# Filler products of the ones matrix in four of TensorE's waits in the delta rule layer

## The chip, the core and the metric

The kernel runs on one NeuronCore of a Trainium2 chip. The metric is the device time of one execution in microseconds (us). PE is TensorE (matrix products), DVE is VectorE, ACT is ScalarE, POOL is GpSimd, SP is the engine that issues the transfers. PSUM has eight banks of 128 partitions x 512 f32 values; PE writes its results there and the other engines read them.

## The reference, cut to what matters

Batch 1, 512 tokens, model width 1024. Three blocks follow each other: a gated delta rule and retention block with an MLP behind it, an attention and pooling block, and a convolution block. The change lies in the first.

```python
n = _rms_norm(h, attn_norm_w)
proj = einsum('bsd,dc->bsc', n, w_in)
(gq, gk, gv, gg, ga, gb, rq, rk, rv, rg) = split(proj)
o_gdn = _gated_deltanet(gq, gk, gv, gg, ga, gb, ...)   # conv, silu, l2norm, then per chunk:
    # m     = strict_lower((k*beta) k^T * decay);  t_mat = (I + m)^-1
    # qk    = (q k^T) * decay
    # u     = t_mat vb - w state;  o = q_dec state + qk u
    # o     = rms(o) * norm_w * silu(gate)
o_ret = _retention(rq, rk, rv, rg)
h = h + concat([o_gdn, o_ret]) @ w_out
```

## The kernel before

Activations are kept by feature, 128 features on the partitions and 512 tokens in a row. A *unit* u is one output tile of 128 features (or, for units 12 to 15, of 128 tokens by 512 columns) of one of the weight matrices, all units of all layers in one numbered list. Units 0 to 31 (U1 to U2) are the projection w_in of the first block, units 32 to 39 (U2 to U3) its w_out. A unit has two halves of four contraction tiles k each. `three` makes an f32 product of a tile from three products of rounded parts (w_hi x_hi, w_hi x_lo, w_lo x_hi), so a unit is 24 products of 128x512, lines 1799, 1800 and 1801. Weights come by DMA into `raw`, ACT rounds them to `w_hi` (line 662) and POOL takes the rest as `w_lo` (line 536), in a ring that PE's finished halves (`half_done`) release.

Everything runs in an order written out by hand for each engine; engines wait for each other by semaphores. The main products go to PSUM banks 0 to 3 (unit u to bank u % 4) and PE waits for `bank_free` before it writes one again. Banks 4 to 7 are for the small products of the delta rule and of retention, which PE does between two units. What matters here:

- After unit 12 (`u == 12`, line 2101) PE waits for `sqk`, ACT's squares of q and k (line 770), and sums them over features with the matrix ONES into banks 4 to 7.
- After unit 15 and after unit 16 (line 2119) it forms k k^T and then k q^T, 16 products of 128x128 each. Ahead of the second it waits for `m_ready`, with which DVE signals that it has read the first out of banks 4 to 7 (line 1382).
- DVE multiplies the second result by the decay (line 1350, `qkt_ready`), and makes the start matrix t of the inversion (lines 1354 and 1355, `t2_ready`). After unit 17 PE waits for both and transposes t (line 2126). ACT copies it (line 804), and six `level` steps between units 18 to 23 build the inverse.
- The tiles of units 12 to 15 are read by DVE at line 1376, with four increments of `bank_free`, ahead of the matrix m.
- The first four units of w_out are interleaved by the rule for QUADS: first the first halves (k = 0 to 3, the retention features) of all four, then the second halves (k = 4 to 7, the delta rule's heads). After the first of the first halves PE sums the squares of the four delta rule heads into banks 4 to 7 (`deltanet_ssq`, line 1823). ACT makes 1/rms of each (lines 859 and 860, one increment of `rr_ready` for each head, after two of the retention part), DVE applies it and the gate (lines 1410, 1414), ACT rounds the operand (line 673, `op_hi`) and DVE takes the rest (line 1180, `op_lo`). The second half of unit 32 waits for `op_hi` and `op_lo` of each k.

The kernel already has, further on at line 2259, 22 products of ONES with itself into bank 6, ahead of the convolution layer.

Of the kernel before, what the change touches and what calls it, by code (L numbers as in the profile page):

```python
# [9 lines left out]
P = 128  # L10
# [4 lines left out]
H = 4  # L15
# [34 lines left out]
U1, U2, U3, U4, U5, U6, U7, U8 = 0, 32, 40, 84, 108, 126, 134, 158  # L50
# [73 lines left out]
def build(nc, a, const, out, x_t):  # L124
    ctx = ExitStack()
    with ctx:
        base = (nc.sbuf_base + 31) // 32 * 32

        def at(name, shape, dt, off):
            return nc.alloc_sbuf_tensor_at(name, shape, dt, offset=base + off)  # L130

        def sem(name):
            return ctx.enter_context(nc.semaphore(name))
# [9 lines left out]
        ONES = at("ones", [P, P], F32, G + 512)  # L143
# [114 lines left out]
        PS = ctx.enter_context(nc.psum_tensor("ps", [P, 8, S], F32))  # L258
# [12 lines left out]
        bank_free = sem("bank_free")  # L271
# [30 lines left out]
        rsq_ready, rssq_filled, rr_ready = sem("ret_sq"), sem("ret_ssq_filled"), sem("ret_rstd")  # L302
# [1486 lines left out]
        def _(pe):  # L1789
            mm, tr = nc.tensor.matmul, nc.tensor.transpose  # L1790
# [6 lines left out]
            def three(out, w_hi_, w_lo_, x_hi_, x_lo_, first, last):  # L1797

                mm(out, w_hi_, x_hi_, start=first, stop=False)  # L1799
                mm(out, w_hi_, x_lo_, start=False, stop=False)  # L1800
                return mm(out, w_lo_, x_hi_, start=False, stop=last)  # L1801

            def half_unit(n, out, X, k0, kn, first, last, fill=None, later=None):


                for s_ in (w_hi, w_lo):
                    pe.wait_ge(s_, n + 1 if later is None else later + (n + 1))
                for k in range(kn):
                    if fill is not None:
                        operand(8 * fill + k0 + k)  # L1810
                    ins = three(out, WH[:, n % 4, k, :], WL[:, n % 4, k, :],
                                X[:, k0 + k, 0, :], X[:, k0 + k, 1, :],
                                first and k == 0, last and k == kn - 1)
                ins.then_inc(half_done, 1)

            def deltanet_ssq():

                pe.wait_ge(tokk_ready, 4)
                pe.wait_ge(tokv_ready, 16)
                pe.wait_ge(o_ready, 4)  # L1820
                for h in range(H):
                    pe.wait_ge(rsq_ready, 1 + h + 1)
                    mm(PS[:, 4 + h, :], ONES[:, :], RR[:, h, :], start=True, stop=True).then_inc(rssq_filled, 1)

            def four_halves(m, X, fill, k0):

                for k in range(2):
                    operand(8 * fill + k0 + k)
                    for j in range(4):
                        if k == 0:  # L1830
                            if k0 == 0:
                                pe.wait_ge(bank_free, m + j - 3)
                            pe.wait_ge(w_hi, 2 * U7 + k0 + j + 1)
                            pe.wait_ge(w_lo, 2 * U7 + k0 + j + 1)
                        three(PS[:, (m + j) % 4, :], WH[:, j, k, :], WL[:, j, k, :],
                              X[:, k0 + k, 0, :], X[:, k0 + k, 1, :], k0 + k == 0, False)
                for j in range(4):
                    if k0 == 4 and j == 3:
                        pre1_stat()
                    for k in range(2, 4):  # L1840
                        if j == 0:
                            operand(8 * fill + k0 + k)
                        ins = three(PS[:, (m + j) % 4, :], WH[:, j, k, :], WL[:, j, k, :],
                                    X[:, k0 + k, 0, :], X[:, k0 + k, 1, :], False, k0 + k == KT - 1)
                    ins.then_inc(half_done, 1)

            def unit(u, m, X, fill=None, later=None, mlater=None, midway=None):
                for q in QUADS:
                    if 0 <= u - q < 4:
                        if u == U7:  # L1850
                            four_halves(m, X, fill, 0)
                            four_halves(m, X, fill, 4)
                        if q == U7:
                            return
                        if u == q:
                            for j in range(4):
                                if m >= 4:
                                    pe.wait_ge(bank_free, m + j - 3)
                                half_unit(2 * q + j, PS[:, (m + j) % 4, :], X, 0, 4, True, False,
                                          fill if j == 0 else None)  # L1860
                                if j == 0 and u == U2:
                                    deltanet_ssq()
                            if midway is not None:
                                stat(midway)
                        half_unit(2 * q + 4 + u - q, PS[:, m % 4, :], X, 4, 4, False, True,
                                  fill if u == q else None)
                        return
                if m >= 4:

                    pe.wait_ge(bank_free, m - 3 if mlater is None else mlater + (m - 3))  # L1870
                out = PS[:, m % 4, :]
                half_unit(2 * u, out, X, 0, 4, True, False, fill, later)
                half_unit(2 * u + 1, out, X, 4, 4, False, True, fill, later)

            def wide_half(n, X, fill=None, last_of=None):

                q0 = max(q for q in WIDE if q <= n // 2)
                k = n - 2 * q0
                m = q0 if q0 < U2 else M8 + q0 - U8
                for s_ in (w_hi, w_lo):  # L1880
                    pe.wait_ge(s_, n + 1)
                if fill is not None:
                    operand(8 * fill + k)
                w, wl = (r[:, n % 4, :, :].rearrange("p t c -> p (t c)") for r in (WH, WL))
                for b in range(NB):
                    if k == 0:
                        pe.wait_ge(bank_free, m + b - 3)
                    xh, xl = (X[:, k, q, b * P:(b + 1) * P] for q in range(2))
                    ins = three(PS[:, (m + b) % 4, :], xh, xl, w, wl, k == 0, k == KT - 1)
                    if k == KT - 1 and b < NB - 1 and last_of is not None:  # L1890
                        ins.then_inc(last_of, 1)
                ins.then_inc(half_done, 1)

            def stat(st):

                pe.wait_ge(acc_done, squares_before(st) + 8)
                mm(PS[:, 7, :], ONES[:, :], ACC[:, :], start=True, stop=True).then_inc(stat_filled, 1)
# [164 lines left out]
            def ret_ssq(r):  # L2062
# [4 lines left out]
                    ins = mm(PS[:, 4 + h, :], ONES[:, :], RR[:, 2 * r + h, :], start=True, stop=True)  # L2067
                ins.then_inc(rssq_filled, 1)

            for u in range(U1, U2):  # L2070
                if 12 <= u < 16:
                    wide_half(2 * u, XA)
                    wide_half(2 * u + 1, XA)
                else:
                    unit(u, u, XA, fill=0 if u == 0 else None, midway=0)
                if u == 3:
                    pe.wait_ge(ab_split, 2)
                    pe.wait_ge(rstd_ready, 1)
                    for k in range(KT):
                        ins = three(PS[0:8, 7, :], ABH[:, k, :], ABL[:, k, :], XA[:, k, 0, :], XA[:, k, 1, :],  # L2080
                                    k == 0, k == KT - 1)
                    ins.then_inc(ab_filled, 1)
# [83 lines left out]
            for k in range(KT):  # L2166
                unit(U2 + k, M2 + k, XA, fill=1 if k == 0 else None)

            unit(U3, M3, XB, fill=2)
            pe.wait_ge(rr_ready, 2 + H)  # L2170
            stat(1)
# [56 lines left out]
            for u in range(U5, U6):  # L2228
                n = u - U5
# [150 lines left out]
```

## Time and profile before

| | us |
|---|---|
| three timed runs | 1213.53, 1218.21, 1221.34 |
| their median | 1218.21 |
| the profiled execution | 1210.9 |
| its span on the core | 1208.8 |
| PE busy | 1153.3 |
| DVE busy | 737.4 |
| POOL busy | 527.3 |
| ACT busy | 463.8 |

All times in the rows are from the profiled execution, counted from the start of its span. A product's duration in a row (0.39 us for 128x512) overlaps with the next one's; what one costs is the distance between two starts. A product of f32 operands that aren't rounded shows as two records. An idle time in square brackets stands with the row that ends it. PEclk is the TensorE clock that was granted, as a share of 2.4 GHz: 1.00 is 2.4 GHz, 0.50 is 1.2 GHz. The mean over this execution is 0.991.

### The profile page before, as it was taken

How to read it: one execution, taken by the hardware profiler on the slowest of the kernel's cores; microseconds unless marked ns; L12 is line 12 of the kernel's file. 1: busy time of each engine (PE TensorE's matmuls, PEld its weight loads, DVE VectorE, ACT ScalarE, POOL GpSimd, SP SyncE). 2: the span in 40 equal slices, each digit the busy share in tenths (PEclk: the TensorE clock that was granted, in tenths of full speed). 3: DMA queues.
4: the chain of work that ended last, by engine and by line, in shares of the span. 5: the costliest groups of instructions: out<-in, count | busy, mean ns of one | idle time of the engine just before them, and what ended most of it. 6: DMA issues, size and time to landing. Idle time of an engine off the chain costs nothing.

```text
span 1208.8 us, 16113 instructions
## 1 busy us (share of the span) xinstructions
PE 1153.3 (95%) x5876; PEld 918.8 (76%) x5876; DVE 737.4 (61%) x948; ACT 463.8 (38%) x812; POOL 527.3 (44%) x376
## 2 busy tenths in 40 slices
PE   5999999999989999999999999999989989999996
PEld 4686778877868777777778888876667768888774
DVE  5796664442356788888883111625764578886963
ACT  4325411215465333232232333434354443343553
POOL 4456520212225455545555444532237367532533
PEclk9999999999999999999999999999999999999998
DMA  8774341205213233233232323422123242122221
GB/s 270 102 88 71 48 57 36 36 1 140 70 35 105 70 105 104 70 103 104 71 103 95 97 96 99 145 71 69 35 70 85 55 123 71 35 71 71 70 70 70
DMA packets 101630, 99.37 MB, mean 82 GB/s; under 512 B 4804, under 2 KB 96069, under 8 KB 101061
## 3 DMA queue, kind: packets, MB, share of 16 engines
q1 hardware_dynamic: 101572, 98.59, 30.4%
q8 instruction: 38, 0.62, 0.2%
q14 instruction: 20, 0.16, 0.0%
HBM read 94.38 MB, written 4.19 MB: 82 GB/s over the span
## 4 chain that ended last, share of the span: by engine, by line
PE 61%; issue 15%; DVE 10%; POOL 9%; ACT 3%; DMA 1%; DVEq 0%; POOLq 0%; SPq 0%; ACTq 0%
PE ps L1799 15%; PE ps L1800 15%; PE ps L1801 15%; POOL w_lo L536 8%; PE ps L2276 4%; PE ps L2006 2%; PE ps L1999 2%; PE ps L2214 1%; PE ps L1968 1%; PE ps L2224 1%; PE ps L1989 1%; DVE conv L1637 1%; DVE v L1233 1%; PE ps L2101 1%; PE ps L1963 1%
## 5 line engine op out<-in xcount | busy, mean ns | idle before, releaser
L536 POOL TENSOR_TENSOR w_lo<-raw,w_hi 128x512 fp32r<-128x512 f32 x332 | 470.0, 1428 | 638.7 <-ACT w_hi L662 638.4
L662 ACT ACTIVATE w_hi<-raw 128x512 fp32r<-128x512 f32 x332 | 197.4, 618 | 231.2 <-PE ps L1801 209.2
L1799 PE MATMUL ps<-x_a,w_hi 128*128 128x512 f32 x624 | 253.1, 406 | 14.5 <-POOL w_lo L536 5.5
L1800 PE MATMUL ps<-x_a,w_hi 128*128 128x512 f32 x624 | 244.8, 392 | 0.0
L1801 PE MATMUL ps<-x_a,w_lo 128*128 128x512 f32 x624 | 244.6, 392 | 0.0
L1799 PE MATMUL ps<-x_b,w_hi 128*128 128x512 f32 x416 | 165.4, 398 | 2.7 <-POOL w_lo L536 1.4
L1801 PE MATMUL ps<-x_b,w_lo 128*128 128x512 f32 x416 | 162.3, 390 | 0.0
L1800 PE MATMUL ps<-x_b,w_hi 128*128 128x512 f32 x416 | 162.0, 389 | 0.0
L1799 PEld LDWEIGHTS ps<-x_a,w_hi 128*128 128x128 f32 x624 | 118.1, 189 | 54.8 <-issue 24.3
L1801 PEld LDWEIGHTS ps<-x_a,w_lo 128*128 128x128 f32 x624 | 118.1, 189 | 25.4
L1800 PEld LDWEIGHTS ps<-x_a,w_hi 128*128 128x128 f32 x624 | 118.3, 190 | 25.0 <-issue 2.2
L1799 PEld LDWEIGHTS ps<-x_b,w_hi 128*128 128x128 f32 x416 | 78.0, 188 | 30.5 <-issue 13.4
L1801 PEld LDWEIGHTS ps<-x_b,w_lo 128*128 128x128 f32 x416 | 78.1, 188 | 16.8
L1800 PEld LDWEIGHTS ps<-x_b,w_hi 128*128 128x128 f32 x416 | 78.1, 188 | 15.5 <-issue 0.2
L1637 DVE TENSOR_TENSOR conv<-ps,conv 32x511 f32<-32x511 f32 (+2 forms) x96 | 65.5, 682 | 17.2 <-ACT conv L1055 14.3
L1450 DVE SCALAR_TENSOR_TENSOR conv_f<-pad_f,mlp_conv,conv_f 128x512 f32<-128x512 f32 x44 | 67.6, 1536 | 6.5 <-DVE conv_f L1449 1.7
L1799 PE MATMUL ps<-mlp_act,w_hi 128*128 128x512 f32 x176 | 68.6, 390 | 0.2 <-POOL w_lo L536 0.2
L1801 PE MATMUL ps<-mlp_act,w_lo 128*128 128x512 f32 x176 | 68.5, 389 | 0.0
L1800 PE MATMUL ps<-mlp_act,w_hi 128*128 128x512 f32 x176 | 68.5, 389 | 0.0
L1472 DVE TENSOR_TENSOR res<-ps,res 128x512 f32<-128x512 f32 x8 | 5.5, 685 | 82.2 <-PE ps L1801 82.2
L1452 DVE SCALAR_TENSOR_TENSOR conv_f<-pad_f,mlp_conv,conv_f 128x512 f32<-128x512 f32 x44 | 51.6, 1173 | 6.3
L900 ACT ACTIVATE mlp_act<-prod_f 128x512 f32 (+1 forms) x22 | 13.9, 632 | 95.2 <-DVE prod_f L1459 95.2
(346 smaller groups left out, 1652.4 us busy)
## 6 DMA issues: line engine op xcount, KB each, us to landing
raw<-in_w_up SPq DMA_DIRECT2D x44, 512.0 KB, 4.3
raw<-in_w_in SPq DMA_DIRECT2D x32, 512.0 KB, 8.0
raw<-in_c_w_in SPq DMA_DIRECT2D x24, 512.0 KB, 4.6
raw<-in_a_w_in SPq DMA_DIRECT2D x18, 512.0 KB, 4.4
raw<-in_w_down SPq DMA_DIRECT2D x16, 512.0 KB, 4.3
raw<-in_w_out SPq DMA_DIRECT2D x8, 512.0 KB, 4.4
raw<-in_c_w_out SPq DMA_DIRECT2D x8, 512.0 KB, 4.2
raw<-in_w_down SPq DMA_DIRECT2D x8, 384.0 KB, 3.4
```

The costliest lines, as they stand in the source:

```text
L536: nc.gpsimd.tensor_tensor(ring_half(WL, n), raw_half(n), f32(ring_half(WH, n)), SUB) \
L662: nc.scalar.activation(ring_half(WH, n), raw_half(n), ACT.Copy).then_inc(w_hi, 1)
L900: nc.scalar.activation(ACTS[:, bass.ds(n + (j - 2), 1), 0, :] .rearrange("p a s -> p (a s)"), PRODF[:, j - 2, :], ACT.Copy) \
L1450: step(v.scalar_tensor_tensor(out=d, in0=x[:, 2:2 + S], scalar=w[1], in1=d, op0=MUL, op1=ADD))
L1452: ins = v.scalar_tensor_tensor(out=d, in0=x[:, 1:1 + S], scalar=w[0], in1=d, op0=MUL, op1=ADD)
L1637: ins = v.tensor_tensor(y, PS[32 * q:32 * q + 32, 4 + r, 0:S - late_by], y, ADD)
L1799: mm(out, w_hi_, x_hi_, start=first, stop=False)
L1800: mm(out, w_hi_, x_lo_, start=False, stop=False)
L1801: return mm(out, w_lo_, x_hi_, start=False, stop=last)
L1999: ins = mm(PS[:, 4 + c, h * 64:(h + 1) * 64], M[:, a_, :], half(TT[:, a_, :], 1), start=True, stop=True)
L2006: ins = mm(PS[:, 4 + c, 256 + h * 64:256 + (h + 1) * 64], T[:, a_, :], half(XZ[:, c, h, :], 1), start=True, stop=True)
L2276: ins = mm(PS[:, 4 + r, :], w, g[p, k % 2, TAP_PHASES * j:TAP_PHASES * j + S], start=first, stop=last)
```

## The change

At four places PE gets products of ONES[128x128] with ONES[128x128] ahead of a wait that it had: nine after unit 12 into bank 4, nine after unit 16 into bank 1, eleven after unit 17 into bank 2, and nine into bank 7 between the first and the second halves of the first four units of w_out. No engine reads the results; the next product into the same bank overwrites them. The two in the banks of main products wait for `bank_free` first, as the next unit does, and the last waits for `rr_ready` to reach 2 + H = 6, since bank 7 holds the fourth head's sum until ACT has taken it.

```diff
--- before.py
+++ after.py
@@ -1860,6 +1860,10 @@
                                           fill if j == 0 else None)
                                 if j == 0 and u == U2:
                                     deltanet_ssq()
+                            if u == U2:
+                                pe.wait_ge(rr_ready, 2 + H)
+                                for _ in range(9):
+                                    mm(PS[:, 7, 0:P], ONES[:, :], ONES[:, :], start=True, stop=True)
                             if midway is not None:
                                 stat(midway)
                         half_unit(2 * q + 4 + u - q, PS[:, m % 4, :], X, 4, 4, False, True,
@@ -2067,12 +2071,21 @@
                     ins = mm(PS[:, 4 + h, :], ONES[:, :], RR[:, 2 * r + h, :], start=True, stop=True)
                 ins.then_inc(rssq_filled, 1)
 
+            def ones_products(n, bank):
+                for _ in range(n):
+                    mm(PS[:, bank, 0:P], ONES[:, :], ONES[:, :], start=True, stop=True)
+
             for u in range(U1, U2):
                 if 12 <= u < 16:
                     wide_half(2 * u, XA)
                     wide_half(2 * u + 1, XA)
                 else:
                     unit(u, u, XA, fill=0 if u == 0 else None, midway=0)
+                if u == 12:
+                    ones_products(9, 4)
+                if u == 16 or u == 17:
+                    pe.wait_ge(bank_free, u + 1 - 3)
+                    ones_products(9 if u == 16 else 11, (u + 1) % 4)
                 if u == 3:
                     pe.wait_ge(ab_split, 2)
                     pe.wait_ge(rstd_ready, 1)
```

Two of the places in PE's own order, since the diff doesn't show what stands around them. In a row: line, operation, what it writes and reads, columns, and in brackets the semaphores that it waits for. `ret_rstd` is the program's name of `rr_ready`. PE between the halves of w_out's first units, with the change:

```order
L1799 MATMUL ps<-x_a,w_hi 128x512
L1800 MATMUL ps<-x_a,w_hi 128x512
L1801 MATMUL ps<-x_a,w_lo 128x512
L1866 MATMUL ps<-ones 128x128 [waits ret_rstd]
L1866 MATMUL ps<-ones 128x128 x8
L1799 MATMUL ps<-x_a,w_hi 128x512 [waits op_hi,op_lo,w_lo_ready,w_hi_ready]
L1800 MATMUL ps<-x_a,w_hi 128x512
L1801 MATMUL ps<-x_a,w_lo 128x512
L1799 MATMUL ps<-x_a,w_hi 128x512 [waits op_lo,op_hi]
```

The second halves of the products, k = 4 and on, now stand behind the nine and behind their wait. PE at the end of unit 17, with the change:

```order
L1801 MATMUL ps<-x_a,w_lo 128x512
L2076 MATMUL ps<-ones 128x128 [waits bank_free]
L2076 MATMUL ps<-ones 128x128 x10
L2139 MATMUL ps<-ident,t 128x128 [waits t2_ready,qkt_ready]
L2139 MATMUL ps<-ident,t 128x128 x15
```

Here the eleven stand ahead of the transposes (line 2126 before, 2139 with the change) and of their wait; nothing else has another place.

## Rows read from the trace of the kernel before

**Rows 1.** The page, busy time of PE, share of the span, instructions.

```profile
PE 1153.3 (95%) x5876; PEld 918.8 (76%) x5876; DVE 737.4 (61%) x948; ACT 463.8 (38%) x812; POOL 527.3 (44%) x376
```

**Rows 2.** Stretches: busy time (x count) by engine, PEclk, DMA share, GB/s.

```profile
core 0: us, PE busy (x) PEld busy (x) DVE busy (x) ACT busy (x) POOL busy (x), PEclk, DMA share, GB/s
104.30:109.50 5.20, 3.15 (x9) 1.48 (x9) 0.72 (x5) 4.22 (x7) 0.00 (x0) 1.00 0.99 151
143.20:145.40 2.20, 0.00 (x0) 0.00 (x0) 2.20 (x2) 0.63 (x1) 2.20 (x3) 1.00 0.00 0
146.60:149.70 3.10, 3.10 (x16) 3.10 (x16) 0.00 (x0) 0.00 (x0) 1.27 (x2) 0.50 0.96 87
149.70:150.60 0.90, 0.90 (x9) 0.90 (x9) 0.00 (x0) 0.00 (x0) 0.00 (x0) 0.95 0.97 96
156.40:159.00 2.60, 0.00 (x0) 0.03 (x1) 2.60 (x2) 0.00 (x0) 0.31 (x1) 1.00 0.79 77
160.00:163.50 3.50, 3.50 (x14) 3.11 (x13) 3.35 (x7) 1.77 (x2) 0.00 (x0) 0.51 0.00 0
356.60:362.00 5.40, 3.26 (x15) 2.55 (x15) 3.35 (x5) 1.93 (x4) 1.42 (x2) 1.00 0.58 194
951.00:958.00 7.00, 6.35 (x50) 5.86 (x49) 5.04 (x6) 3.67 (x6) 2.30 (x2) 1.00 0.01 2
```

**Rows 3.** Timeline of PE at full clock: start us, us, engine, line, what.

```profile
134.00 3.73 PE L2119 MATMUL ps<-kq 128*128 128x128 f32 x32
137.49 0.48 PE L1799 MATMUL ps<-x_a,w_hi 128*128 128x512 f32 x1
...
174.93 0.48 PE L1799 MATMUL ps<-x_a,w_hi 128*128 128x512 f32 x1
...
176.40 0.40 PE L1799 MATMUL ps<-x_a,w_hi 128*128 128x512 f32 x1
...
180.51 1.91 PE L1989 MATMUL ps<-ident,tt 128*128 128x128 f32 x16
182.25 3.68 PE L1999 MATMUL ps<-tt,m 128*128 128x64 f32 x32
...
951.15 5.07 PE L2259 MATMUL ps<-ones 128*128 128x128 f32 x44
```

**Rows 4.** Timeline of PE, ahead of and behind the first three waits.

```profile
103.86 0.39 PE L1801 MATMUL ps<-w_hi,x_a 128*128 128x512 f32 x1
106.34 3.70 PE L2101 MATMUL ps<-sq,ones 128*128 128x512 f32 x8 [2.09 <-ACT sq L770]
...
142.80 0.39 PE L1801 MATMUL ps<-x_a,w_lo 128*128 128x512 f32 x1
145.45 5.47 PE L2119 MATMUL ps<-kq 128*128 128x128 f32 x32 [2.26 <-DVE m L1382]
150.67 0.47 PE L1799 MATMUL ps<-x_a,w_hi 128*128 128x512 f32 x1
...
155.99 0.39 PE L1801 MATMUL ps<-x_a,w_lo 128*128 128x512 f32 x1
159.01 2.68 PE L2126 MATMUL ps<-ident,t 128*128 128x128 f32 x16 [2.63 <-DVE t L1355]
161.34 0.77 PE L1799 MATMUL ps<-x_a,w_hi 128*128 128x512 f32 x1
...
163.78 0.39 PE L1799 MATMUL ps<-x_a,w_hi 128*128 128x512 f32 x1
```

**Rows 5.** Timeline of DVE, the reads of the banks of units 12 to 15.

```profile
135.33 2.72 DVE L1376 TENSOR_SCALAR ret_v<-ps,rstd_col 128x512 f32<-128x512 f32 x4
```

**Rows 6.** Timeline at the second halves of w_out: ACT, PE and DVE.

```profile
354.21 0.63 ACT L860 ACTIVATE rr<-rr 128x512 f32<-128x512 f32 x1
354.90 0.39 PE L1799 MATMUL ps<-x_a,w_hi 128*128 128x512 f32 x1
...
357.91 1.47 DVE L1180 SCALAR_TENSOR_TENSOR x_a<-kq,x_a 128x512 fp32r<-128x512 f32 x2
358.75 0.47 PE L1799 MATMUL ps<-x_a,w_hi 128*128 128x512 f32 x1 [2.14 <-ACT x_a L673]
```

## The prediction

> **What bounds the kernel now.** I read the page's busy times first, then TensorE's (PE's) waits, then the granted clock around the long waits, then the rows of PE, DVE and ACT at the four places that the change touches. PE is busy for 1153.3 of 1208.8 us [rows 1], so it sets the end, and every microsecond that it loses or wins in a row of its own goes through to the end unless a later wait absorbs it. The four places that the change touches are waits of it [rows 4, 6]: 2.09 us for ACT's squares of q and k (call it place A, unit 12), 2.26 us for DVE's matrix m (B, unit 16), 2.63 us for DVE's matrix t (C, unit 17), and 2.14 us for the x_a operand after the gated norm (D, first unit of the output projection). In each of them PE stands while another engine works through a chain. The change puts products inside the waits; it doesn't shorten what is waited for. So nothing can come from the 9.1 us of waiting itself.
>
> What can come is the clock. The stretches of [rows 2] show it: at A and D the granted clock stays at 1.00 (2.4 GHz) during and behind the wait. At B the wait of 2.2 us is followed by 3.1 us at 0.50 (1.2 GHz), at C the wait of 2.6 us by 3.5 us at 0.51. (At A and D the stretch of the row holds the wait and some 3 us behind it.) The fall comes about 1 us after PE has started again, so the whole of it is paid in PE's own rows.
>
> **The change, part by part.** It adds 38 products of 128x128 by 128x128 (9, 9, 11, 9) and three waits ahead of them, and removes nothing.
>
> *Price of one product.* The kernel already has 22 such products: 44 records (an f32 product takes two) in 5.07 us, all at clock 1.00 [rows 2, 3]. 5.07 / 44 = 0.115 us for a record, so nine products take 18 x 0.115 = 2.07 us and eleven 22 x 0.115 = 2.53 us.
>
> *Are they hidden?* A: PE's last product before the wait starts at 103.86 [rows 4] and products of this form start 0.23 us apart, so the nine run from 104.09 to 106.16; the wait ended at 106.34. Spare 0.18 us. B: last start 142.80, so 143.03 + 2.07 = 145.10 against 145.45, spare 0.35. C: last start 155.99, so 156.22 + 2.53 = 158.75 against 159.01, spare 0.26. All three cost nothing, because ACT's and DVE's work covers them; without that cover they would cost their 2.07 or 2.53 us.
>
> *The added waits.* B and C wait for bank_free at 14 and at 15. The increments 13 to 16 come from DVE's four rows at L1376, which start at 135.33 and take 2.72 us together [rows 5]: done at 138.05, 5 us before PE comes to B. Price nothing. D waits until rr_ready has reached 6, which is ACT's fourth exponential at L860, 354.21 + 0.63 = 354.84 [rows 6]. PE reaches that point at 354.90: the start of k = 4 of the second half, which needs only the first head's operand. So this wait costs 0 to 0.1 us. Behind it stand the nine products, to 357.0, and only then k = 4 and k = 5, which before ran in the same gap (six products: six starts 0.23 us apart, with up to 0.1 us more where k = 5 waits anew, 1.5 us). They end at 357.0 + 1.5 = 358.5. The next row, k = 6, waited until 358.75 for DVE's L1180 (start 357.91). Spare 0.2 us, cost nothing. No other engine's work hangs on k = 4 and k = 5 alone, since the half's end is signalled after k = 7.
>
> *What the clock gives back at B.* The 32 records of L2119 take from 145.45 to the next row's start at 150.67, 5.22 us; the same 32 at unit 15 take 134.00 to 137.49, 3.49 us, at full clock [rows 3, 4]. Saving 1.73 us. DVE's L1350 starts on the end of these, and L1354 and L1355, for which C waits, follow it without a gap; so C's wait ends 1.73 us earlier too and stays as long as it was. The saving goes through.
>
> *What it gives back at C.* The 16 transposes of L2126 take 2.33 us to the next row's start, the 16 of L1989 at full clock 1.74: 0.59 us. The six products behind them take 161.34 to 163.78, 2.44 us, and six at full clock 174.93 to 176.40, 1.47 us: 0.97 us [rows 3, 4]. Saving 1.56 us. Behind it PE runs without a gap to the levels, whose DVE work is started by PE's own rows; short waits on DVE there move with PE. The weights' splits are released by PE's finished halves and move as well.
>
> *Do these products hold the clock?* Through the 22 of them, from 951 us on, and 2 us behind, the clock stayed at 1.00 [rows 2, 3]. At B it even rose again, to 0.95 as a mean from 149.7 us on, while PE ran only L2119, 128x128 f32 records of the same shape. I take it that they do. That they only help in part is bounded by nothing regained (0) and all (3.29).
>
> The Trainium skill (TensorE: Matmul & The Clock Gate, Why this matters for your kernels) warns only of idle gaps that are longer than any of these four. By that rule none of the four waits would let the clock fall, and the change would be worth 0 instead of 3.3 us. This trace disagrees at B (2.3 us) and C (2.6 us), and I go by the trace; but the gaps at A and D (2.1 us) agree with it.
>
> *Sum.* 1.73 + 1.56 + 0 + 0 = 3.3 us. The profiled execution took 1210.9 us, so with the change 1207.6. That execution is 7.3 us quicker than the median of the three timed runs (1218.2) and quicker than all of them, so I carry the saving over to the median: 1218.2 - 3.3 = 1214.9 us.
>
> **The rivals.**
>
> *More falls than the profile shows.* The waits at A and D are only 0.2 us shorter than B's, and the clock fell at one and not at the others; the runs of before span 7.8 us. If in the usual run it falls at A and D as well, the change saves there what B or C show, 1.6 us each: 6.5 us in all, 1211.7 us. Against it: both are at 1.00 throughout here.
>
> *No gain.* The clock falls at B and C regardless, or falls at A or D instead, since the products fill a wait only to within 0.2 to 0.35 us and short waits stay beside them; or the falls of this profile aren't there in the usual run. Time as before, 1218. For it: at A and D gaps nearly as long did nothing. Against it: the stretch from 951 us. (It is also where the skill's rule above leads.)
>
> *Slower: the products outlast the waits.* If the clock is low when PE reaches them, they take longer than the spare. The same shape at 0.50 gave 16 records in 3.10 us [rows 2], 0.194 us each: nine products 3.49, eleven 4.26 us, and over their spare by 1.24 (A), 1.07 (B), 1.47 (C) and 1.2 (D), 5.0 us, so 1223.2 us. The 76 records must cost over 0.128 us each for a loss where nothing is regained (the spares are 0.99 us in all), and over 0.171 where the 3.3 us are. Against it: ahead of all four the clock is at 1.00, PE having run full. A late sixth rr_ready at D would cost the same way, microsecond for microsecond beyond 0.2 us.
>
> **How the numbers follow.** Forecast as summed: 0.60; more falls removed: 0.15; no gain: 0.18; slower: 0.07. The forecast is the first, 1214.9 us. The median of three runs of before lies between 1213.5 and 1221.3, so each case has some 4 us on either side. The range from the second case less most of that, 1207, to the no-gain case with some of it, 1221, leaves out about 2 in 10. A measurement of this kernel can hardly tell 1%, 12 us, from no change, and no case reaches that: the largest gain is 6.5 us, the largest loss 5.0. Within 1%: 0.95; faster by more: 0.03, where a low set of runs meets the second case; slower by more: 0.02.
>
> **What the profile of the changed kernel would show.** Granted clock 1.00 from 143 to 166 us, the second L2119 group at 3.5 us and the L2126 group at 1.9 us: right on the clock. Waits ahead of L2101, L2119, L2126 no longer than 0.4 us, and their start unmoved against ACT's or DVE's row that releases them (0.05 to 0.15 us behind its end): right on the cover. If such a row starts over 0.2 us behind its releaser's end, the products outlast the wait. At D the wait for k = 6 shrinks to 0.2 us with k = 6 still right behind L1180. The forecast is wrong if the clock still falls at B or C, if it falls at other places more often than before, or if the difference is larger than the places A to D can hold.

## The result

| | before | with the change |
|---|---|---|
| median of the runs of the first set, us | 1218.02 (7 runs) | 1208.85 (7 runs) |
| ratio, 95% interval | 1 | 0.9945 (0.9926 to 0.9964) |
| profiled execution, us | 1210.9 | 1208.08 |
| its span, us | 1208.8 | 1206.0 |
| its mean granted clock | 0.991 | 0.994 |
| median of a second set on one chip, us | 1213.91 (35 runs) | 1209.56 (12 runs) |
| ratio, 95% interval | 1 | 0.9974 (0.9962 to 0.9987) |

One of the seven runs of the change in the first set was disturbed (1765.6 us): the median of the first row has it (without it 1208.7), the ratio and the table further on don't. The ratio is estimated over the single runs and isn't the quotient of the two medians, which is 0.9925 in the first set (9.2 us) and 0.9964 in the second (4.4 us). The kernel is a little faster: 6.7 us (4.4 to 9.0) by the first ratio, 3.2 us (1.6 to 4.6) by the second, against 3.3 us forecast. Both are inside 1%.

The busy times on the page of the changed kernel answer to [rows 1]: PE has 76 records more and 5 us more of busy time in a shorter span.

```profile
PE 1158.4 (96%) x5952; PEld 924.8 (77%) x5952; DVE 738.9 (61%) x948; ACT 463.8 (38%) x812; POOL 528.3 (44%) x376
```

The granted clock in stretches around the four places, with the change. The columns are those of [rows 2]; the clock is the third number from the end. The last two rows are the wait in the first units of the convolution layer, which the change leaves alone.

```profile
104.60:106.80 2.20, 2.19 (x19) 1.98 (x17) 0.00 (x0) 2.20 (x2) 0.00 (x0) 1.00 0.97 135
106.80:110.00 3.20, 3.12 (x8) 1.45 (x9) 0.69 (x4) 2.25 (x6) 0.00 (x0) 1.00 1.00 166
143.70:145.90 2.20, 2.01 (x18) 1.81 (x17) 2.20 (x2) 0.63 (x1) 2.20 (x3) 1.00 0.03 7
145.90:149.50 3.60, 3.55 (x31) 3.55 (x32) 0.09 (x1) 0.00 (x0) 2.50 (x3) 1.00 0.68 56
154.90:157.90 3.00, 2.85 (x25) 2.65 (x23) 3.00 (x2) 0.00 (x0) 0.69 (x1) 1.00 1.03 82
157.90:163.00 5.10, 5.10 (x31) 4.52 (x32) 4.88 (x10) 2.72 (x3) 0.66 (x1) 1.00 0.20 24
352.20:354.30 2.10, 2.10 (x20) 2.06 (x19) 2.10 (x3) 1.03 (x2) 1.27 (x1) 1.00 0.00 0
354.30:361.00 6.70, 6.54 (x29) 4.96 (x29) 3.41 (x6) 3.44 (x6) 1.89 (x2) 1.00 0.48 157
966.90:969.40 2.50, 0.17 (x1) 0.00 (x0) 2.50 (x3) 2.50 (x5) 1.54 (x2) 0.99 1.04 301
969.80:972.50 2.70, 2.63 (x6) 1.64 (x6) 2.36 (x3) 0.30 (x1) 1.21 (x1) 0.50 0.21 51
```

The clock is at 1.00 behind all four, where it was 0.50 and 0.51 behind B and C. Behind the wait that isn't filled it still falls.

PE's timeline at the four places, with the change, against [rows 4] and [rows 6]: start, duration, what, and in brackets the idle time ahead.

```profile
104.62 2.17 PE L2076 MATMUL ps<-ones 128*128 128x128 f32 x18
106.88 3.70 PE L2114 MATMUL ps<-sq,ones 128*128 128x512 f32 x8
...
143.54 2.17 PE L2076 MATMUL ps<-ones 128*128 128x128 f32 x18
145.95 3.84 PE L2132 MATMUL ps<-kq 128*128 128x128 f32 x32 [0.25 <-DVE m L1382]
149.55 0.48 PE L1799 MATMUL ps<-x_a,w_hi 128*128 128x512 f32 x1
...
155.12 2.62 PE L2076 MATMUL ps<-ones 128*128 128x128 f32 x22
157.89 1.94 PE L2139 MATMUL ps<-ident,t 128*128 128x128 f32 x16
159.58 0.48 PE L1799 MATMUL ps<-x_a,w_hi 128*128 128x512 f32 x1
...
161.06 0.39 PE L1799 MATMUL ps<-x_a,w_hi 128*128 128x512 f32 x1
...
352.24 2.27 PE L1866 MATMUL ps<-ones 128*128 128x128 f32 x18
354.27 0.48 PE L1799 MATMUL ps<-x_a,w_hi 128*128 128x512 f32 x1
...
356.07 0.47 PE L1799 MATMUL ps<-x_a,w_hi 128*128 128x512 f32 x1 [0.16 <-ACT x_a L673]
```

Follow one event through both traces. The row that ends wait A starts at 106.34 before and at 106.88 now: this execution is 0.54 us behind for reasons of its start and its weights (the first unit's products begin at 20.19 and not 19.91). The row that ends wait B: 145.45 and 145.95, still half a microsecond behind. The first product behind L2119: 150.67 and 149.55. The transposes: 159.01 and 157.89, that is, wait C has moved along. The seventh product behind them: 163.78 and 161.06. The end of wait D: 358.75 and 356.07. The span's end: 1208.8 and 1206.0. From 0.5 us behind to 2.8 ahead are 3.3 us, and 3.2 of them are won between the ends of wait B and 164 us.

### The profile page after: what moved, and what is told of

Read it like the earlier page. It is cut to its first block, busy times and chain, and to the rows that moved or that the text cites. A ratio compares the mean times of both kernels' runs of the same rounds, so it can differ in the third digit from the quotient of the medians.

```text
span 1206.0 us, 16265 instructions
## 1 busy us (share of the span) xinstructions
PE 1158.4 (96%) x5952; PEld 924.8 (77%) x5952; DVE 738.9 (61%) x948; ACT 463.8 (38%) x812; POOL 528.3 (44%) x376
## 4 chain that ended last, share of the span: by engine, by line
PE 61%; issue 15%; DVE 11%; POOL 9%; ACT 3%; DMA 1%; DVEq 0%; POOLq 0%; SPq 0%; ACTq 0%
PE ps L1799 15%; PE ps L1801 14%; PE ps L1800 14%; POOL w_lo L536 8%; PE ps L2289 4%; PE ps L2010 2%; PE ps L2003 2%; PE ps L2227 1%; PE ps L1972 1%; PE ps L2237 1%; PE ps L1993 1%; DVE conv L1637 1%; DVE v L1233 1%; DVE x_a L1180 1%; ACT x_a L673 1%
## 5 line engine op out<-in xcount | busy, mean ns | idle before, releaser
L536 POOL TENSOR_TENSOR w_lo<-raw,w_hi 128x512 fp32r<-128x512 f32 x332 | 471.0, 1431 | 634.4 <-ACT w_hi L662 634.1
L900 ACT ACTIVATE mlp_act<-prod_f 128x512 f32 (+1 forms) x22 | 13.9, 633 | 95.2 <-DVE prod_f L1459 95.2
```

The lines of the kernel that those rows point to most:

```text
L536: nc.gpsimd.tensor_tensor(ring_half(WL, n), raw_half(n), f32(ring_half(WH, n)), SUB) \
L900: nc.scalar.activation(ACTS[:, bass.ds(n + (j - 2), 1), 0, :] .rearrange("p a s -> p (a s)"), PRODF[:, j - 2, :], ACT.Copy) \
```

## Where the rest of the gain comes from: the parts

In the profiled pair the gain is what was forecast; the ratio of the first set shows twice that. Each timed run comes with its mean granted clock, so a set shows how much its runs lose to it: (1 - mean clock) x span. The table has all kernels of this study; the last column is the mean time less what is lost to the clock. A tail of some 8 us, where PE has finished and the clock is low, is in every row and costs nothing.

| kernel | runs | mean us | mean clock | lost to the clock, us | the rest, us |
|---|---|---|---|---|---|
| before, set of the first four | 35 | 1214.8 | 0.9886 | 13.9 | 1200.9 |
| before, set of the last four | 35 | 1214.0 | 0.9894 | 12.8 | 1201.2 |
| the change, first set | 6 | 1209.3 | 0.9928 | 8.7 | 1200.7 |
| the change again | 12 | 1210.4 | 0.9924 | 9.2 | 1201.2 |
| B and C only | 12 | 1212.5 | 0.9908 | 11.1 | 1201.4 |
| A and D only | 12 | 1212.8 | 0.9909 | 11.0 | 1201.8 |
| D only | 12 | 1214.9 | 0.9896 | 12.6 | 1202.3 |
| half of the products | 12 | 1211.1 | 0.9912 | 10.7 | 1200.4 |
| the waits only | 12 | 1215.4 | 0.9880 | 14.6 | 1200.9 |
| twice the products | 12 | 1218.0 | 0.9918 | 10.0 | 1208.0 |
| six places | 12 | 1211.4 | 0.9953 | 5.6 | 1205.7 |

The three theories that the first four runs were to tell apart: (1) the clock falls at A and D as well, in other executions than the profiled one; (2) all of the gain comes from B and C; (3) the part beyond 3.3 us is scatter between sets.

**B and C only.** The edit, against the changed kernel:

```diff
-                            if u == U2:
-                                pe.wait_ge(rr_ready, 2 + H)
-                                for _ in range(9):
-                                    mm(PS[:, 7, 0:P], ONES[:, :], ONES[:, :], start=True, stop=True)
...
-                if u == 12:
-                    ones_products(9, 4)
```

> Filler products only after units 16 and 17 (places B and C), none after unit 12 and none between the halves of w_out. The change as a whole measured 0.9945 of before, 6.7 us, twice the 3.3 us that the profile of before shows for B and C. Theory 1 (in the usual run of before the clock falls at A and D as well): this kernel saves only its own share, about 3.3 us, ratio 0.997, and the granted clock is below 1.00 behind A or D in its profile or in the mean clock of its runs. Theory 2 (all of it comes from B and C, and a fall there costs more in the usual run than in the profiled one): ratio 0.9945 here. Theory 3 (the extra 3.4 us are scatter between sets of runs): 0.997 here and 0.997 for the whole change when measured again.

Measured: 0.9983 (0.9968 to 0.9998), 2.1 us. Its profile shows the fall at D, where the profile of before has none. Stretches of 2 us behind wait D:

```profile
356.00:358.00 2.00, 0.91 (x3) 0.64 (x4) 1.63 (x3) 1.15 (x2) 0.40 (x1) 0.92 0.81 279
358.00:360.00 2.00, 2.00 (x6) 1.62 (x6) 0.47 (x1) 0.00 (x0) 0.87 (x1) 0.50 0.71 246
360.00:362.00 2.00, 2.00 (x8) 1.54 (x8) 0.22 (x1) 1.74 (x4) 0.00 (x0) 0.73 0.00 0
```

Theory 2 is out: the place that was whole in one execution is not whole in the next, and B and C alone don't bring 0.9945.

**A and D only.** The edit takes out the filler after units 16 and 17 instead.

```diff
-                if u == 16 or u == 17:
-                    pe.wait_ge(bank_free, u + 1 - 3)
-                    ones_products(9 if u == 16 else 11, (u + 1) % 4)
```

> Filler products only after unit 12 and between the halves of w_out (places A and D), none after units 16 and 17. Theory 1 (the clock falls at A and D as well in the usual run of before): about 3.3 us saved, ratio 0.997, with the clock at 0.50 behind B and C in the profile. Theory 2 (all from B and C) and theory 3 (scatter): no change, ratio 1.000, since the profile of before has clock 1.00 at A and D.

Measured: 0.9985 (0.9969 to 1.0000), 1.8 us, and 2.9 us less lost to the clock than in before. Theories 2 and 3 expected 1.000, at the interval's very end; the time alone hardly excludes it, but the clock does, since both means in that difference have a standard error of 0.4 us. In its profile the clock falls at C (0.52 from 160 to 162 us) but not at B, which is as empty there as before:

```profile
146.00:150.00 4.00, 3.94 (x34) 3.90 (x35) 0.15 (x3) 0.00 (x0) 2.49 (x3) 1.00 0.63 67
158.00:160.00 2.00, 2.00 (x12) 2.00 (x13) 1.89 (x5) 0.00 (x0) 0.00 (x0) 0.63 0.62 66
160.00:162.00 2.00, 2.00 (x9) 1.81 (x8) 1.96 (x4) 0.80 (x1) 0.00 (x0) 0.52 0.00 0
```

**The whole change again**, unchanged, beside the last four kernels.

> The whole change once more, unchanged, so that it stands beside its parts on one chip. B and C alone gave 0.9983, A and D alone 0.9985, and half of the products at all four 0.9974, in a set where before had a median of 1214.5 us (1218.0 in the first set). If the parts add up, 0.9968; the 0.9945 of the first set then holds some 2.7 us of scatter between sets. If the four places help each other, 0.9945 again. The mean granted clock of before's 35 runs was 0.9886, that is 13.9 us lost to the clock, and that of the whole change's six 0.9928, 8.7 us lost; theory 1 (the clock falls at any of the four, now at one and now at another) expects that difference, about 5 us, in the clock of this set too.

Measured: 0.9974 (0.9962 to 0.9987), 3.2 us, and 3.6 us less lost to the clock. The parts gave 2.1 and 1.8 us, 3.9 together, measured against before in their own set: they add up within their intervals, of some 1.8 us each way. The 6.7 us of the first set don't come back. Its before ran at a median of 1218.0 us and both later ones at 1214.5 and 1213.9, so most of the difference lies in the runs of before; the first set had seven of them. Theory 3 is right on that.

**The waits only.** All three added waits, none of the products.

```diff
                 if u == 16 or u == 17:
                     pe.wait_ge(bank_free, u + 1 - 3)
-                    ones_products(9 if u == 16 else 11, (u + 1) % 4)
...
                             if u == U2:
                                 pe.wait_ge(rr_ready, 2 + H)
-                                for _ in range(9):
-                                    mm(PS[:, 7, 0:P], ONES[:, :], ONES[:, :], start=True, stop=True)
```

> The three added waits (bank_free at 14 and at 15, rr_ready at 6) without any of the products. Priced at nothing, nothing and 0 to 0.1 us: ratio 1.000. If the waits themselves cost or gain (through the order in which PE takes up its queue), it lies off 1.000 by more than the interval.

Measured: 1.0011 (0.9995 to 1.0027). The waits cost nothing that can be told, and bring nothing: the gain is the products'. Its profile is the clearest for theory 1. With all four places empty it shows the fall at three of them, A, C and D, and none at B. Stretches of 2 us behind A, B, C and D:

```profile
108.00:110.00 2.00, 2.00 (x3) 0.68 (x2) 1.27 (x5) 0.53 (x3) 0.41 (x1) 0.50 0.88 137
...
148.00:150.00 2.00, 2.00 (x20) 2.00 (x20) 0.00 (x0) 0.00 (x0) 1.51 (x2) 1.00 0.90 81
...
160.00:162.00 2.00, 2.00 (x11) 2.00 (x10) 1.93 (x4) 0.00 (x0) 0.00 (x0) 0.50 0.14 34
...
360.00:362.00 2.00, 2.00 (x6) 1.52 (x7) 0.51 (x1) 0.31 (x1) 1.28 (x1) 0.58 1.08 378
```

**D only.** A and the pair B and C are taken out of the changed kernel.

> Filler products only between the halves of w_out (place D). A and D together gave 1.8 us, and in the profiles seen so far without a filler at A the clock never fell there, while at D it fell in one. If D carries the pair: ratio 0.9985. If both fall equally often: 0.9993. The granted clock at B or C is below 1.00 in its profile.

Measured: 1.0007 (0.9993 to 1.0020), neither of the two expected; 0.9985 is excluded, 0.9993 lies at the interval's end. Its profile shows the clock fall at A and at B, and C whole. How the gain splits between A and D stays open: 12 runs with a standard error of 0.7 us can't settle 0.8 us. Beyond the falls at A and B its profiled execution is late for two reasons that have nothing to do with the fillers. One weight tile arrives late, ACT rounds it ahead of the copy of uu in its fixed order, and PE waits for uu:

```profile
290.85 0.63 ACT L662 ACTIVATE w_hi<-raw 128x512 fp32r<-128x512 f32 x1 [4.68 <-DMA raw<-in_w_in]
292.02 1.16 PE L2055 MATMUL ps<-qkt,uu 128*128 128x128 f32 x8 [1.39 <-ACT uu L719]
```

In before's profile that tile is there early enough and PE doesn't wait at this place. The wait stands in six of the ten profiles, at 0.9 to 3.0 us (waits only 0.87, B and C only 1.01, six places 1.35, D only 1.39, half 1.44, twice 2.99), so it is likely one source of the scatter in the last column of the table; no timed run shows it. The other reason is a fall of the clock at 883 us, behind two waits of 1.54 and 1.11 us in the attention layer.

Put together, by the profiles (+ the clock fell behind the empty wait, - it didn't, f filled and it didn't):

```
                      A   B   C   D
before                -   +   +   -
the waits only        +   -   +   +
D only                +   +   -   f
A and D only          f   -   +   f
B and C only          -   f   f   +
the change, twice     f   f   f   f
half, twice, six      f   f   f   f
```

Of 15 empty waits 9 have a fall behind them, at each place in some profile and not in another; of 25 filled ones none (four of the 25 are the half-filled ones of the next section). At 1.6 us a fall (B's 1.73 and C's 1.56 in the prediction), four places with 9 chances in 15 each are 3.9 us in the mean: the 3.2 us of the second set and the 3.9 us of the parts fit. That the profile of before had two falls, where 2.4 is the average, was luck, and by it the forecast from that one profile came out near the mean.

The clock also fell twice outside these places: at 883 us in D only, as said, and at 294 us in the kernel with twice the products, at the end of its wait of 2.99 us for uu.

## How much product is needed, and what too much costs

**Half the products**, 4, 4, 5 and 4.

```diff
-                    ones_products(9, 4)
+                    ones_products(4, 4)
...
-                    ones_products(9 if u == 16 else 11, (u + 1) % 4)
+                    ones_products(4 if u == 16 else 5, (u + 1) % 4)
...
-                                for _ in range(9):
+                                for _ in range(4):
```

> All four places, with 4, 4, 5 and 4 products in place of 9, 9, 11 and 9, which leaves some 1.2 to 1.4 us of each wait empty. If what counts is that no wait of over 2 us stays empty, the clock is held and the ratio is that of the whole change, 0.9945, all the products beyond being of no use. If the clock needs the wait filled to the end, it falls at some of the four and the ratio lies between 0.9945 and 1.000.

Measured: 0.9974 (0.9959 to 0.9989), the same as the whole change in the second set. Its waits, from the list of PE's waits:

```profile
PE ps L2139 <- DVE t L1355: 1.5, 1, 1.5
PE ps L2132 <- DVE m L1382: 1.4, 1, 1.4
PE ps L1799 <- ACT x_a L673: 1.3, 1, 1.3
PE ps L2114 <- ACT sq L770: 1.2, 1, 1.2
```

With 1.2 to 1.5 us of each wait left empty the clock stayed at 1.00 behind all four in its profile. At a chance of 9 in 15 each, four in a row without a fall would come in 3 profiles of 100. It isn't shown that so short a rest is always safe: the fall at 883 us in D only came behind waits of that length, two in close succession. Its 12 runs lose 10.7 us to the clock and the whole change's 9.2 and 8.7, so a fall now and then may remain; the times don't tell the two apart.

**Twice the products**, 18, 18, 22 and 18.

> All four places with 18, 18, 22 and 18 products. The sum of the prediction prices a record at 0.115 us and the spare of the four waits at 0.18, 0.35, 0.26 and 0.2 us. If that is right the second lot is uncovered: 2.07 - 0.18 + 2.07 - 0.35 + 2.53 - 0.26 + 2.07 - 0.2 = 7.75 us more than with the change, so a ratio of 0.9945 + 0.0064 = 1.001. If the records are cheaper where PE is late, or a later wait takes up what is lost (the chain of ACT and DVE behind D, or the weights), less: 0.997 or below.

Measured: 1.0029 (1.0015 to 1.0043). Against the whole change's 0.9974 these are 6.7 us more, and 7.0 us in the table's column without the clock, where 7.75 were expected. PE's and its releasers' rows at A, B, C and D:

```profile
104.10 4.18 PE L2076 MATMUL ps<-ones 128*128 128x128 f32 x36
104.42 1.90 ACT L770 ACTIVATE sq<-kq 128x2048 f32<-128x2048 f32 x1
108.11 3.60 PE L2114 MATMUL ps<-sq,ones 128*128 128x512 f32 x8
...
144.67 4.18 PE L2076 MATMUL ps<-ones 128*128 128x128 f32 x36
144.76 2.29 DVE L1382 TENSOR_TENSOR m<-ps,m 128x2048 f32<-128x2048 f32 x1
148.69 3.51 PE L2132 MATMUL ps<-kq 128*128 128x128 f32 x30
...
157.11 3.25 DVE L1355 SCALAR_TENSOR_TENSOR t<-t,ident 128x2048 f32<-128x2048 f32 x1
157.72 5.07 PE L2076 MATMUL ps<-ones 128*128 128x128 f32 x44
162.63 1.91 PE L2139 MATMUL ps<-ident,t 128*128 128x128 f32 x16
...
364.56 0.63 ACT L673 ACTIVATE x_a<-kq 128x512 fp32r<-128x512 f32 x1 [2.14 <-DVE kq L1414]
366.94 0.39 PE L1799 MATMUL ps<-x_a,w_hi 128*128 128x512 f32 x1
```

ACT's squares end at 106.32 and PE's row starts at 108.11: 1.8 us late; at B it is 148.69 against 147.05, 1.6 us; at C 162.63 against 160.36, 2.3 us; at D the product of k = 6 starts at 366.94, where ACT had its operand ready at 365.19, 1.7 us. Together that is 7.4 us, between the 7.75 expected and the 7.0 of the table. Everything beyond the wait's end is paid. Each record takes (108.11 - 104.10) / 36 = 0.111 us from start to start, a little less than the 0.115 that the prediction used, since that had the last record's tail in it.

## A filled wait that brings nothing

Two long waits are left behind which the clock fell in every profile where they weren't filled: ahead of the first unit (4.2 us, then 3.4 us or more at 0.50) and in the first units of the convolution layer. If the rule held everywhere, filling them would give another 3.2 us.

```diff
             for k in range(4, KT):
                 x_tile(k)
+            for _ in range(14):
+                mm(PS[:, 3, 0:P], ONES[:, :], ONES[:, :], start=True, stop=True)
             pe.wait_ge(par_ready, 4)
...
                     for j in range(4):
+                        if k0 == 4 and k == 0 and j == 2:
+                            for _ in range(9):
+                                mm(PS[:, 6, 0:P], ONES[:, :], ONES[:, :], start=True, stop=True)
```

> The whole change and two more fillers, in the two other long waits of PE behind which the clock falls in every profile so far: 14 products ahead of the first unit (a wait of 4.2 us, then some 3.4 us at 0.50) and 9 in the wait of 2.4 us for POOL's w_lo in the first units of the convolution layer (then some 3 us at 0.50). If a filled wait keeps the clock wherever it is, both low stretches go, 1.6 us each: 3.2 us less than the whole change, ratio about 0.994 where that has 0.997, and the mean clock of the runs rises by 0.0027. If the first unit's products are then held by the weights (POOL's w_lo) anyway, only the second counts, 1.6 us. If the product count is too large for the wait at the start, which varies with the first transfers, part of the gain is lost.

Measured: 0.9980 (0.9969 to 0.9991), no better than the four places. The clock did what was expected: 0.9953 in the mean, 3.5 us less lost, and in its profile at 1.00 throughout but for the tail. The time went into the next waits, and the trace shows which. PE at the first units, first with four places, then with six:

```profile
20.19 0.54 PE L1799 MATMUL ps<-x_a,w_hi 128*128 128x512 f32 x1 [4.18 <-issue]
25.21 0.47 PE L1799 MATMUL ps<-x_a,w_hi 128*128 128x512 f32 x1 [0.45 <-POOL w_lo L536]
```

```profile
20.19 0.47 PE L1799 MATMUL ps<-x_a,w_hi 128*128 128x512 f32 x1 [1.42 <-issue]
25.21 0.47 PE L1799 MATMUL ps<-x_a,w_hi 128*128 128x512 f32 x1 [1.89 <-POOL w_lo L536]
```

The same product starts at 25.21 in both. At full clock PE is through 1.44 us sooner and waits 1.44 us longer for POOL's w_lo. In the convolution layer it is DVE's sum of squares. PE's row that ends the next wait there, with six places:

```profile
982.27 1.13 PE L1916 MATMUL ps<-acc,ones 128*128 128x512 f32 x2 [1.82 <-DVE acc L1596]
```

With four places no idle time stands ahead of that row. There DVE's chain and the cold PE ended together. And DVE's chain itself took longer. DVE and POOL there, first with four places, then with six:

```profile
974.41 5.30 DVE L1596 TENSOR_TENSOR acc<-acc,sq 128x512 f32<-128x512 f32 x6
977.74 3.10 POOL L536 TENSOR_TENSOR w_lo<-raw,w_hi 128x512 fp32r<-128x512 f32 x2 [6.73 <-ACT w_hi L662]
```

```profile
975.98 6.24 DVE L1596 TENSOR_TENSOR acc<-acc,sq 128x512 f32<-128x512 f32 x6
978.54 3.13 POOL L536 TENSOR_TENSOR w_lo<-raw,w_hi 128x512 fp32r<-128x512 f32 x2 [5.96 <-ACT w_hi L662]
```

A PE that is through sooner releases the weights sooner, so POOL's rows start 2.6 us behind the start of DVE's six additions and no longer 3.3, and more of the additions run beside them. The six take 4.33 us where POOL hardly overlaps them (the whole change again, half, D only, A and D only), 5.3 with four places and 6.24 with six. From PE's restart behind the wait for w_lo to the row for DVE's sum it is 10.3 us with four places (969.47 to 979.76) and 11.2 with six (971.04 to 982.27), although PE's clock is whole there with six and not with four. The profiled execution with six places ends 2.5 us later than the one with four: 0.9 us come from here, and 1.35 of the rest is its wait for uu. How the 4.5 us by which the two differ in the table's last column divide in the timed runs isn't shown beyond that.

## Why the prediction was right, and where it was thin

- **The clock behind B and C**: right. Sized 1.73 and 1.56 us; in the profile 5.22 us became 3.60 (145.95 to 149.55), 1.62 us, and 2.33 us became 1.69 (157.89 to 159.58), 0.64 us, with 1.0 us more in the six products behind (2.44 us became 1.48, 159.58 to 161.06). The whole, 3.3 us, is what the two traces differ by.
- **That it goes through**: right. Wait C moved along with L2119, and the end of wait D and of the span are ahead by as much as PE was at 164 us. The chain at these places hangs on PE's own rows. The six places show the opposite, where it hangs on POOL or DVE.
- **The cover**: right. Idle 0.25 us is left at B, under 0.2 at A and C, 0.16 at D, and the ends of A's, B's and C's waits stand where their releasers put them.
- **The added waits at nothing**: right by the waits only, 1.0011 with 1.000 inside the interval, and at D by the rows: ACT's fourth exponential ended at 352.19 and the products started at 352.24.
- **The rule of the Trainium skill** on idle gaps that the prediction cites (TensorE: Matmul & The Clock Gate, Why this matters for your kernels), by which there would be no gain: the trace and the runs decide against reading it as a safe limit, with nine falls behind gaps of 2.1 to 2.6 us.
- **The rival of more falls** was not a rival but the same thing seen over many executions: A and D fall too, and B and C don't always. The prediction gave A and D a price of 0 because one profile had the clock at 1.00 there. That step was wrong, and so was the certainty of B and C; that the two errors cancelled in the sum is luck. The rival's own sum, 6.5 us from falls at all four, is too high by the same count of 9 in 15.
- **The level**: the forecast of 1214.9 us rested on the median of three runs, 1218.2. The 70 later runs of before have their medians at 1214.5 and 1213.9, so the profiled execution's 1210.9 was 3 to 4 us low and not 7; 2 to 3 of these go with its clock (0.991, 10.9 us lost, against 13.9 and 12.8 in the mean). The measured 1208.85 is 6 us under the forecast. Against the later sets 4 of the 6 are the level. In its own set, where before's median was 1218.02, all 6 are a larger gain, 9.2 us between the medians where 3.3 were forecast; why that set's before ran high isn't shown.
- **Twice the products** confirmed the slower rival's working, though not its condition: what runs over a wait is paid in full, also at full clock.

## What to carry to other kernels

A wait of PE of 2 us, and once two of 1.5 and 1.1, can be followed by a stretch at half the clock, and whether it is in one execution says little of the next: look at several profiles, or at the mean clock of the runs, before a place is priced at zero or at full. Products into a free bank hold the clock at the price of nothing as long as they end inside the wait; half the wait's length did as well here as all of it, and leaves room for the wait to shrink. The gain counts only where the work behind the wait is what sets the end: where another engine's chain is due at the same time, as POOL's and DVE's at the two added places, it turns into idle time. An engine that gets ahead also moves the others' work: at the second added place POOL's rows came to lie beside DVE's, and DVE's chain grew by 0.9 us.

## What the runs showed of the hardware

- Behind the same idle wait of 2.1 to 2.6 us of TensorE the granted clock fell to 0.50 in 9 cases of 15 and stayed at 1.00 in 6. The fall began anywhere from the restart itself (the waits only, at C: clock low from 158.9, restart at 159.08) to 1.4 us behind it (D only at A and B: 108.2 and 149.2 against 107.00 and 147.80), and cost 1.6 us.
- Products of a constant matrix with itself, whose result nobody reads, kept the clock like any other: 25 filled waits, no fall, four of them filled to a half only.
- Of before's scatter between executions, 1210.7 to 1220.0 us, a part goes with the clock: the mean clock of its runs goes from 0.985 to 0.992, and in the 35 runs of the first four the time falls by 0.6 us for each microsecond less that the formula counts as lost (correlation 0.61).
- One of DVE's additions (L1596, 128x512) takes 0.69 us, and 1.67 us where it runs beside POOL's w_lo (L536). Of the six additions the longer time is seen in none in the second profile of the whole change, in one in the first and in two with six places.
